# Cached keys loaded as token pairs on 128 partitions, with one full-width copy for four half-width ones

## What is computed

```python
def compress_blocks(kseq, pe, w1, w2):
    ...
    ch = kp.reshape(B, nc, CMP_STRIDE, KH, HD).transpose(0, 1, 3, 2, 4).reshape(B, nc, KH, CMP_STRIDE * HD)
    ha = ch @ w1[:half]
    hb = ch @ w1[half:]
    h = ha[:, :-1] + hb[:, 1:] + pe.reshape(-1) @ w1
    return jax.nn.silu(h) @ w2
```

## Time and profile before

| what | value |
|---|---|
| median of 3 runs | 3194.33 us (3194.32 to 3202.76) |
| profiled execution: span, which is its own time here | 3193.5 us |
| TensorE / VectorE / ScalarE busy | 2825.2 / 1059.6 / 657.4 us |
| mean granted TensorE clock | 0.899 |
| page transfers of the scores stages (`cache`) | 512, 192 KB each |
| page transfers of the attention stages (`vsel`) | 384 on SP and 128 on ScalarE, 64 KB each |

### The profile page before, as it was taken

One profiled execution on the slowest core, in us unless ns is written; L12 is line 12 of the kernel. 1 busy time (PEld: TensorE's weight loads), 2 busy tenths in 40 slices (PEclk: granted clock), 3 DMA queues, 4 the chain that ended last, 5 costly groups with the idle time before them and its releaser, 6 DMA issues. The chain is left out here.

```text
span 3193.5 us, 40852 instructions
## 1 busy us (share of the span) xinstructions
PE 2825.2 (88%) x14496; PEld 2243.3 (70%) x14496; DVE 1059.6 (33%) x2571; ACT 657.4 (21%) x1514; POOL 226.7 (7%) x228
## 2 busy tenths in 40 slices
PE   6997999699698799999869889996978987999996
PEld 4876777466585588888658767765657765888885
DVE  1823555344543201000128244554444322100002
ACT  0023444223310100000011244442232102000001
POOL 0500000000030100000105000000002101000000
PEclk8997999799696899999979979997987878999998
DMA  6214555143001222222052165532420012222220
GB/s 189 67 46 147 176 185 171 51 116 96 2 21 45 66 77 71 76 69 67 1 144 66 41 200 173 164 122 81 121 62 1 21 47 86 73 67 76 69 53 28
DMA packets 334996, 274.00 MB, mean 86 GB/s; under 512 B 52865, under 2 KB 330562, under 8 KB 334458
## 3 DMA queue, kind: packets, MB, share of 16 engines
q1 hardware_dynamic: 300072, 247.38, 26.1%
q10 hardware_dynamic: 34770, 24.55, 2.6%
HBM read 262.01 MB, written 18.17 MB: 88 GB/s over the span
## 5 line engine op out<-in xcount | busy, mean ns | idle before, releaser
L370 PE MATMUL psum<-xT,up_ring 128*128 128x272 f32 x2048 | 473.7, 395 | 21.7 <-PEq L161 21.7
L370 PEld LDWEIGHTS psum<-xT,up_ring 128*128 128x128 f32 x2048 | 391.6, 191 | 104.4 <-issue 23.1
L370 PE MATMUL psum<-ff,HT 128*128 128x272 f32 x1536 | 356.5, 395 | 4.2 <-PEq L161 4.2
L370 PEld LDWEIGHTS psum<-ff,HT 128*128 128x128 f32 x1536 | 294.0, 192 | 66.1 <-issue 5.0
L370 PE MATMUL psum<-xT,w_ring 128*128 128x272 f32 x1408 | 329.1, 397 | 5.2 <-PEq L161 4.0
L370 PEld LDWEIGHTS psum<-xT,w_ring 128*128 128x128 f32 x1408 | 270.8, 193 | 63.4 <-issue 4.7
L1019 PE MATMUL psum<-chunks,W 128*128 128x512 f32 x512 | 240.4, 631 | 10.6 <-DVE chunks L1141 10.6
L1141 DVE COPY chunks<-psum 64x256 f32<-64x256 f32 x512 | 215.1, 420 | 33.5 <-PE psum L998 26.2
L2143 DVE SCALAR_TENSOR_TENSOR xT<-xT,psum 128x544 f32<-128x544 f32 x32 | 23.1, 721 | 592.8 <-PE psum L370 592.8
L998 PE MATMUL psum<-cst,cache 128*128 128x128 f32 x1536 | 199.1, 283 | 20.7 <-DMA cache<-in_cache_nsa_kv 20.7
L998 PEld LDWEIGHTS psum<-cst,cache 128*128 128x128 f32 x1536 | 183.4, 150 | 29.8 <-DMA cache<-in_cache_nsa_kv 22.4
(11 more groups left out here) (415 smaller groups left out, 3283.6 us busy)
## 6 DMA issues: line engine op xcount, KB each, us to landing
cache<-in_cache_nsa_kv SPq DMA_DIRECT2D x512, 192.0 KB, 3.3
up_ring<-in_w_up SPq DMA_DIRECT2D x32, 1024.0 KB, 5.3
vsel<-in_cache_nsa_kv SPq DMA_DIRECT2D x384, 64.0 KB, 2.0
w_ring<-in_w_in SPq DMA_DIRECT2D x20, 1024.0 KB, 5.3
HT<-in_w_down SPq DMA_DIRECT2D x10, 2048.0 KB, 9.1
vsel<-in_cache_nsa_kv ACTq DMA_DIRECT2D x128, 64.0 KB, 2.2
HT<-in_w_out SPq DMA_DIRECT2D x8, 1024.0 KB, 5.9
yT<-in_w_down SPq DMA_DIRECT2D x4, 2048.0 KB, 12.3
```

What stands on the lines that cost most here:

```text
L370: last = pe.matmul(psum[0:w.shape[1], 2 * (t % 4) + h, 0:HALF], w, moving(k)[:, h * HALF:(h + 1) * HALF], start=(k == 0), stop=(k == kt - 1))
```

## The change

A page now arrives in three transfers. Its 128 tokens are split in 64 pairs, and a pair goes to one partition: pages with even numbers within the group to partitions 0 to 63, those with odd ones to 64 to 127. For each of the two tokens of a pair one transfer brings compressed keys and values (4 pieces of 64 floats, laid so that the two tokens' channels of a head are neighbours) into `cmp_in`; a third brings both tokens' selected keys into `sel_in`. The `loaded` counts are three times as high. The transposes read these tiles; after them the partitions of a bank hold (token of the pair, channel), and one copy of 128x512 moves a bank to `chunks`. The columns of the selected scores now run in another order within two pages (first the even tokens of both, then the odd ones), so the block bias is added in two instructions per batch, the nearest bias goes through other access patterns, its table is permuted, and `fetch` lands `v_sel` in the same order: one transfer of 64 partitions x 2 rows of 512 B per page.

```diff
@@ -104,7 +104,7 @@
     t["line"] = one_hot(511 - np.arange(LINE))
     e = np.zeros((33, NT, 416), np.float32)
     for q in range(NT):
-        e[:, q, 0:128] = one_hot(128 + q - np.arange(128), 31)
+        e[:, q, 0:128] = one_hot(128 + q - np.arange(128).reshape(64, 2).T, 31)
         e[:, q, 128:160] = one_hot(q - np.arange(NS) % NT)
         e[:, q, 160:415] = one_hot(PAST + q - 16 * np.arange(NCB) - 31)
         e[31, q, 415] = 1
@@ -935,7 +935,8 @@
     with ExitStack() as c:
         slots, gp = 4, 4
         NG = NPG // gp
-        cache = sb("cache", [P, slots, gp, 3 * P], ctx=c)
+        cmp_in = sb("cmp_in", [P, slots, gp // 2, 2 * KVH, 2, HD], ctx=c)
+        sel_in = sb("sel_in", [P, slots, gp // 2, 2, P], ctx=c)
         chunks = sb("chunks", [P, 2, KVH, 8, NCH], ctx=c)
         kt = sb("kt", [P, 2, gp * P], ctx=c)
         hb = sb("hb", [HD, 2, KVH, NCB], ctx=c)
@@ -954,12 +955,12 @@
             def cols(b):
                 return ds(b * 16, 16)
 
-            def pairs(bank, k, i):
-
-                return psum[HD * k:HD * k + HD, bank, :].rearrange("p (n j i) -> p i j n", j=8, i=2)[:, i]
-
-            def pairs_to(c, k, i, g):
-                return chunks[HD * i:HD * i + HD, c, k, :, g * 32:g * 32 + 32]
+            def pairs(bank):
+
+                return psum[:, bank, :].rearrange("p (k n j) -> p k j n", k=KVH, j=8)
+
+            def pairs_to(c, g):
+                return chunks[:, c, :, :, g * 32:g * 32 + 32]
 
             @block.sync
             def _(sp):
@@ -971,8 +972,12 @@
                             numbers = page_numbers(S, mybir.EngineType.SP, b, g * gp, 2 * gp)
                         for j in range(gp):
                             page = numbers[(g % 2) * gp + j]
-                            src = layer(io.cache_nsa_kv, l)[ds(page, 1)].rearrange("a t c k d -> (a t) (c k d)")
-                            sp.dma_start(cache[:, g % slots, j, :], src[:, 0:3 * P]).then_inc(loaded[g % slots], 16)
+                            src = layer(io.cache_nsa_kv, l)[ds(page, 1)].rearrange("a (p i) c k d -> (a p) i (c k d)", i=2)
+                            r = slice(64 * (j % 2), 64 * (j % 2) + 64)
+                            for i in range(2):
+                                to = cmp_in[r, g % slots, j // 2, :, i, :]
+                                sp.dma_start(to, src[:, i, 0:2 * P].rearrange("p (c d) -> p c d", d=HD)).then_inc(loaded[g % slots], 16)
+                            sp.dma_start(sel_in[r, g % slots, j // 2, :, :], src[:, :, 2 * P:3 * P]).then_inc(loaded[g % slots], 16)
                         if g == 0:
                             if not first:
                                 sp.wait_ge(s.w_turned, b)
@@ -986,17 +991,22 @@
             @block.tensor
             def _(pe):
                 def turn(b, g, first):
-                    pe.wait_ge(loaded[g % slots], b * (16 * gp * NG // slots) + 16 * gp * (g // slots + 1))
+                    pe.wait_ge(loaded[g % slots], b * (48 * gp * NG // slots) + 48 * gp * (g // slots + 1))
                     if not first or g >= 2:
                         pe.wait_ge(s.k_copied, b * NG + (g - 1))
                         pe.wait_ge(s.v_copied, b * NG + (g - 1))
                         pe.wait_ge(s.sel_dve if g % 2 else s.sel_act, b * (NG // 2) + g // 2)
                     if not first and g == 0:
                         pe.wait_ge(s.added, b * 4 - 2)
-                    for c in (2, 0, 1):
-                        for j in range(gp):
-                            last = pe.transpose(psum[:, 3 * (g % 2) + c, j * P:j * P + P],
-                                                cache[:, g % slots, j, c * P:c * P + P], C["ident"])
+                    for j in range(gp):
+                        last = pe.transpose(psum[:, 3 * (g % 2) + 2, j * P:j * P + P],
+                                            sel_in[:, g % slots, j // 2, j % 2, :], C["ident"])
+                    for c in range(2):
+                        for k in range(KVH):
+                            for j in range(gp // 2):
+                                at = (2 * k + j) * P
+                                last = pe.transpose(psum[:, 3 * (g % 2) + c, at:at + P],
+                                                    cmp_in[:, g % slots, j, KVH * c + k, :, :].rearrange("p i d -> p (i d)"), C["ident"])
                     last.then_inc(s.turned, 1)
 
                 def score(b, g, first):
@@ -1095,10 +1105,7 @@
                             act.copy(kt[:, 0, :], psum[:, 2, :]).then_inc(s.sel_act, 1)
                         if not first and g == 0:
                             act.wait_ge(s.summed, b * 2)
-                        for k in range(KVH):
-                            for i in range(2):
-                                last = act.copy(pairs_to(0, k, i, g), pairs(3 * (g % 2), k, i))
-                        last.then_inc(s.k_copied, 1)
+                        act.copy(pairs_to(0, g), pairs(3 * (g % 2))).then_inc(s.k_copied, 1)
                         if g == 1 and not first:
                             vc_out(before)
                     for n, c in enumerate((1, 0)):
@@ -1136,10 +1143,7 @@
                             dve.tensor_copy(kt[:, 1, :], psum[:, 5, :]).then_inc(s.sel_dve, 1)
                         if not first and g == 0:
                             dve.wait_ge(s.summed, b * 2)
-                        for k in range(KVH):
-                            for i in range(2):
-                                last = dve.tensor_copy(pairs_to(1, k, i, g), pairs(3 * (g % 2) + 1, k, i))
-                        last.then_inc(s.v_copied, 1)
+                        dve.tensor_copy(pairs_to(1, g), pairs(3 * (g % 2) + 1)).then_inc(s.v_copied, 1)
                         if g == 1 and not first:
                             kc_out(before)
                         if g == 2 and not first:
@@ -1272,17 +1276,22 @@
             step = Serial(dve, s.step)
             for q in range(NQ):
                 dve.wait_ge(s.turned, q + 1)
-                dve.tensor_tensor(p_sel[:, 512 * q:512 * q + 512].rearrange("p (j n) -> p j n", n=64),
-                                  psum[:, q % 4, :].rearrange("p (j n) -> p j n", n=64), bc(block_bias[:, 8 * q:8 * q + 8], 64),
-                                  ALU.add).then_inc(s.added, 1)
+                for j in range(2):
+                    at = slice(256 * j, 256 * j + 256)
+                    blocks = bc(bc_mid(block_bias[:, 8 * q + 4 * j:8 * q + 4 * j + 4], 2), 32)
+                    last = dve.tensor_tensor(p_sel[:, 512 * q + 256 * j:512 * q + 256 * j + 256].rearrange("p (i j n) -> p i j n", i=2, n=32),
+                                             psum[:, q % 4, at].rearrange("p (i j n) -> p i j n", i=2, n=32), blocks, ALU.add)
+                last.then_inc(s.added, 1)
             dve.wait_ge(s.turned, NQ + 1)
             dve.tensor_scalar(p_win[:, 0:512], psum[:, NQ % 4, :], far, None, ALU.add).then_inc(s.added, 1)
             dve.wait_ge(s.new_scored, 2)
             dve.tensor_tensor(p_sel[:, PAST:], psum[:, 4, 0:NS], new, ALU.add).then_inc(s.new_added, 1)
             dve.tensor_tensor(p_win[:, 512:], psum[:, 5, 0:NS], new, ALU.add).then_inc(s.new_added, 1)
             dve.wait_ge(s.added, NQ + 1)
-            dve.tensor_tensor(p_sel[:, PAST - P:PAST], p_sel[:, PAST - P:PAST], near, ALU.add).then_inc(s.new_added, 1)
-            dve.tensor_tensor(p_win[:, 384:512], p_win[:, 384:512], near, ALU.add).then_inc(s.new_added, 1)
+            last_page = p_sel[:, PAST - 2 * P:PAST].rearrange("p (i a n) -> p i a n", i=2, a=2)[:, :, 1, :]
+            dve.tensor_tensor(last_page, last_page, near.rearrange("p (i n) -> p i n", i=2), ALU.add).then_inc(s.new_added, 1)
+            last_win = p_win[:, 384:512].rearrange("p (n i) -> p i n", i=2)
+            dve.tensor_tensor(last_win, last_win, near.rearrange("p (i n) -> p i n", i=2), ALU.add).then_inc(s.new_added, 1)
             dve.tensor_tensor(p_win[:, 0:NT], p_win[:, 0:NT], C["win_old"], ALU.add).then_inc(s.new_added, 1)
             dve.wait_ge(s.new_added, 5)
             dve.tensor_reduce(stat[:, 1, 0:1], p_sel[:, :], AX.X, ALU.max, negate=True).then_inc(s.maxed, 1)
@@ -1350,8 +1359,10 @@
         def fetch(eng, kind, b, h, first_page, loaded):
 
             for j, page in enumerate(page_numbers(S, kind, b, half * h + first_page, 4)):
-                src = layer(io.cache_nsa_kv, l)[ds(page, 1)].rearrange("a t c k d -> (a t) (c k d)")
-                eng.dma_start(vsel[:, h, first_page + j, :], src[:, 3 * P:4 * P]).then_inc(loaded, 16)
+                src = layer(io.cache_nsa_kv, l)[ds(page, 1)].rearrange("a (p i) c k d -> (a p) i (c k d)", i=2)
+                r = slice(64 * (j % 2), 64 * (j % 2) + 64)
+                t = first_page + j - j % 2
+                eng.dma_start(vsel[r, h, t:t + 2, :], src[:, :, 3 * P:4 * P]).then_inc(loaded, 16)
 
         @block.sync
         def _(sp):
```

## The result

The changed kernel takes **3966.18 us** (median of 4 runs, 3962.45 to 3968.66) against 3198.55 for the kernel before, run beside it: ratio 1.2402 [1.2378, 1.2426], slower by 767.6 us. Its profiled span is 3960.5 us, 767.0 more than the 3193.5 of before, so the two traces account for the whole difference. The forecast was 4010, within 3600 to 4210. The mean granted clock fell from 0.899 to 0.807.

What follows compares the result with a forecast made beforehand. TensorE was taken to bound the scores stage before, SP's issue queue after. 3193.5 + 732 (scores stages) + 86 (attention) + 2 (softmax) = 4013, given as 4010 us, range 3600 to 4210.

Steps and rivals of the forecast that it cites:

- The bound and its move: Scores stage: TensorE bounds at 35.3 us a sequence; SP's queue becomes the bound at 80, 45 us more.
- Price of an issue: Page transfers on SP: 0.60 us each, ends 0.384 and 0.70; a page 2.41 us, a sequence 80.
- The dear rival: Page transfers: an issue costs 0.70 us, as for the `state` store; 4206 us in all, chance 0.15.
- Slots: Scores stage: SP's wait for `turned` to refill one of four slots is empty with SP behind; cost 0.
- Layer: Scores stage, first page transfer to next stage: ends at 949 against 583 us, +366 a layer, +732 in all.
- Attention: Attention stage `fetch`: 24 dearer issues add 6.4 us a sequence, 1.0 absorbed by SP's wait; 5.4 x 16 sequences, +86 us.
- the forecast's own range: Whole kernel: 3900 us (512 B transfers at the flat 0.47) to 4120, around 4010; chance of the forecast 0.65.
- The purse isn't paid: Scores stage: the 11 us from faster copies are not gained, for TensorE no longer sets the pace.
- That is the purse: Scores stage: TensorE's 8 waits for half-width copies, 5.3 us a layer, 11 in all, are what faster copies can gain.
- the rival that was to end faster: Scores stage: SP keeps up, TensorE stays the bound and its waits for copies go; 3185 us, chance 0.03.
- Data: Page transfers in smaller pieces: 29 us a sequence at 226 GB/s, under 35.3 and 80; cost 0 beside the issue.
- Softmax: Softmax: 8 additions of 512 columns become 16 of 256, 1.2 us a layer; +2 us.

Runs made afterwards that it cites:

- run 3: Changed kernel, with the third transfer of each page (selected keys, `sel_in`) issued by GpSimd instead of SyncE: 3608.0 us, ratio 1.1296.
- run 1: Kernel before, with each page in three flat transfers of 128 partitions x 512 B instead of one of 1,536 B: 3531.0 us, ratio 1.1055.
- run 2: Kernel before, with each page in two flat transfers of 64 partitions x 1,536 B: 3409.9 us, ratio 1.0675.
- run 4: Changed kernel, with its three transfers per page dealt out evenly, 48 each a sequence, between SyncE and GpSimd: 3419.4 us, ratio 1.0703.
- run 7: Kernel before, with only the attention stage's `fetch` changed to 64 partitions x 2 rows of 512 B per page: 3247.9 us, ratio 1.0167.
- run 8: Changed kernel, with half-width copies again, four of 64x256 for one of 128x512 on each engine: 3971.4 us, ratio 1.2427.
- run 9: Kernel before, with only the copies changed, one 128x512 for four half-width ones on both engines: 3165.4 us, ratio 0.99.
- run 10: Kernel before, loads and half-width copies kept; hidden product takes the keys first and waits for VectorE's copies of the values only behind them: 3162.7 us, ratio 0.9902.
- run 5: Kernel before, still one transfer per page on 128 partitions, but in six padded 256 B pieces per token: 3228.5 us, ratio 1.0108.
- run 6: Kernel before, with one transfer per page onto 64 partitions as token pairs, 2 rows of 1,536 B: 3226.8 us, ratio 1.0093.

## Why the prediction was right

**The bound and its move.** TensorE before, SP's queue after: right, and shown three ways, by SP's back-to-back issues, by the lost waits and by run 3, which moves a third of the issues and leaves the bytes as they are. TensorE waits 33 us a sequence (265.4 / 8) for the 45 forecast, since its own work takes 14 us a sequence longer at the lower clock (396 us for 286).

**Price of an issue.** 0.60 for all three was taken from the rows with 64 partitions, two levels and 256 B pieces. The two compressed transfers took 0.599, the 512 B one 0.548; between them lay 0.18 to 0.24. A page took 2.37 us for the 2.41 of the sum, a sequence 80.04 for 80. The dear rival (0.70, the price of the store) did not occur. That the sequence came out within 0.1 us is luck, for two errors cancel. The page was 0.04 us too dear, 1.3 us a sequence. The loads of page numbers were too cheap: the sum took 0.55 for each of four, and in the steady sequence from 521.6 to 601.6 us the distance across them is 1.50, 1.51, 1.64 and 1.89 us for the usual 0.79, so 3.4 us for 2.2. The third of them:

```profile
570.40 0.55 SPq L980 DMA_DIRECT2D sel_in<-in_cache_nsa_kv  x1
572.04 1.42 SPq L979 DMA_DIRECT2D cmp_in<-in_cache_nsa_kv  x2
```

The same 1.2 us is most of what the sums of runs 1 to 3 were short, 1.5 to 2.7 us a sequence: in run 1 the four take 1.28, 1.28, 1.43 and 1.65 us for the usual 0.57.

**Slots.** "That wait is empty" held: SP has no wait for TensorE in the changed kernel's stage. It holds at this pace alone; in run 4, at 46 us a sequence, it is 20.1 us in layer 0.

**Layer.** +358 and +357 for +366. The sum added 27.0 us of tail, and 8.5 for long issues, landing and a cold clock. Measured is 667.3 - 8 x 80.04 = 27.0 in all: 2.4 for the landing, as forecast, and 24.6 of tail (912.66 to 937.24), for the tail of before already had a pause and a slow hidden product in it. The 3 us for long issues and the 3 us for the clock were not there.

**Attention.** The step "each issue costs 0.60 - 0.333 more" was mis-sized. These are the transfers of 512 B rows, and they cost 537 ns at the least, as the flat row of 64 partitions (0.468) hinted for the form without small pieces; 24 x 0.2 = 4.9 us a sequence, and the pitch grew by 4.1. Less the 1.0 us that SP waited, 16 sequences give 62. So +57 for +86; run 7 has +51. The lower end of the forecast's own range, with all 512 B transfers at the flat 0.47, had this case in it: 0.13 us less for each of 32 `sel_in` and 24 `vsel` issues a sequence is 117 us, near the 110 from 4010 to 3900.

**Copies.** "The purse isn't paid" was right (run 8). "That is the purse" was wrong: the step put the price of a wait at its own length. The pauses of 5.3 us a layer cost 13.7 in layer 0 and 19.9 in layer 1 by the traces, and 31 and 34 us in all by the medians (runs 9 and 10), for the granted clock behind them falls. Nothing in the answer hung on it, as the issues dwarf it, but the rival that was to end faster was given at 3185 and would have been about 3163, with the fetch still at no cost.

**Data.** "Cost 0 beside the issue" held: DMA share 0.33, within the 0.3 to 0.4 forecast, and 80 / 0.33 = 242 GB/s at a full share, near the 226 assumed. As a general price the 226 was too high for 256 B pieces in a full queue (178 in run 5), and a second cost was missed: landing as pairs on 64 partitions, in pieces as long as before, raised the share from 0.52 to 0.70 (run 6). Where the issue kept up, as in runs 5 and 6, these cost 36 and 30 us.

**Softmax.** +0.6 us for +2; the stage's 39 us hardly depend on the additions.

The sum: 4013 forecast over a span of 3193.5 is +820; measured +767. Of the 53 too many, attention explains 29, the layers 17, softmax 1.4, and 5 are the time that came back in unchanged stages.

## What to carry to other kernels

Before a layout splits a transfer, count the instructions of the queue that issues it, at the price of their own shape (all partitions or half, flat or in pieces), and compare with the time of the loop. Here 32 issues became 96 and filled 80 us of a 35 us loop. Here a profile that said "waits for DMA" at a DMA share of 0.33, with an issuing queue that had no wait of its own, meant the issuer. And before an engine is made faster to remove a short wait, try to reorder the waiting instruction's work, so that what is ready goes first: it gave the whole gain here with no new layout. A pause of TensorE may be worth more than its length, through the clock.

## What was not expected of the hardware

- Half the partitions make an issue dearer, not cheaper: 0.469 us for 0.333, flat rows of the same length (run 2), and 0.537 to 0.548 with two rows, 0.599 with four pieces of 256 B. GpSimd needed 0.585 for the transfer that took SP 0.548 (run 3).
- The same bytes in pieces of the same length kept the DMA engines busy for longer when a page landed as pairs on 64 partitions: share 0.70 at 166 GB/s for 0.52 at 163 (run 6). With one row to each of 64 partitions it was 0.47 at 134 (run 2).
- A pause of 0.66 us in a stretch that is otherwise full was followed, in 10 of 16 cases, by a product 1.56 to 1.70 us longer, with the granted clock at or near 0.50 at its start (0.50 in 1988 to 1991 us); without the pause in none of 16 (run 10).
